# Attention in an encoder layer: probabilities turned in pairs of key blocks, four value products in a row, two banks for the summed output

## The reference

```python
def one(qblk):
    s = jnp.einsum('bqhd,bkhd->bhqk', qblk, k, preferred_element_type=jnp.float32) * scale
    p = jax.nn.softmax(s, axis=-1).astype(v.dtype)
    return jnp.einsum('bhqk,bkhd->bqhd', p, v)
...
a = _dense_attention_blocks(q, k, v)
mla_out = a.reshape(B, S, MLA_WIDTH) * jax.nn.silu(mg)
```

## Time and profile before

| | |
|---|---|
| median of 3 executions | 2474.99 us (2474.07 to 2484.44) |
| the profiled execution | 2480.64 us, of which 2478.5 us are its span |
| TensorE matmul, busy | 2292.8 us, 93% of the span |
| TensorE weight load | 1895.0 us, 76% |
| VectorE | 1399.8 us, 56% |
| ScalarE | 1137.2 us, 46% |
| GpSimd | 1020.0 us, 41% |
| DMA | mean 109 GB/s |
| TensorE's granted clock, mean | 0.975 of full speed |

### The profile page before, as it was taken

How to read it: one execution, slowest core, us unless ns; L and a number is a source line. 1 busy time by engine, 2 the same in 40 slices (tenths; PEclk the granted TensorE clock), 3 DMA queues, 4 the chain that set the end, 5 groups by cost and what they waited for, 6 DMA issues and landing times. The chain is left out here.

```text
span 2478.5 us, 34465 instructions
## 1 busy us (share of the span) xinstructions
PE 2292.8 (93%) x11362; PEld 1895.0 (76%) x11362; DVE 1399.8 (56%) x2120; ACT 1137.2 (46%) x2119; POOL 1020.0 (41%) x754
## 2 busy tenths in 40 slices
PE   1999999999996999999999889988999999996998
PEld 1888878898884787777778668877878888775786
DVE  8333335444345777776777631124888888764342
ACT  3544433222224555555555525553556555552332
POOL 5322222222223333232332212231888988873453
PEclk9999999999998999999999989999999999997999
DMA  7443324343435333333423223330111111124553
GB/s 283 146 151 127 127 84 159 122 144 128 148 118 142 97 109 97 102 97 95 111 84 94 94 99 118 127 110 19 43 52 60 60 58 49 56 111 127 168 149 115
DMA packets 195091, 271.19 MB, mean 109 GB/s; under 512 B 10404, under 2 KB 137764, under 8 KB 190374
## 3 DMA queue, kind: packets, MB, share of 16 engines
q1 hardware_dynamic: 190374, 261.49, 32.9%
q10 hardware_dynamic: 4608, 8.39, 0.9%
HBM read 183.33 MB, written 86.51 MB: 109 GB/s over the span
## 5 line engine op out<-in xcount | busy, mean ns | idle before, releaser
L2141 POOL TENSOR_TENSOR conv_g<-conv_g,product 128x1024 f32<-128x1024 f32 x160 | 380.3, 2413 | 44.8 <-ACT product L2180 44.8
L2270 DVE SCALAR_TENSOR_TENSOR ps_b<-u,cols,ps_b 128x1024 f32<-128x1024 f32 x304 | 364.7, 1281 | 0.0
L2330 PE MATMUL ps_a<-ho_hi,wp_lo 128*128 128x512 f32 x768 | 308.9, 402 | 21.6 <-DVE h_left L2289 6.4
L2332 PE MATMUL ps_a<-ho_hi,wp_hi 128*128 128x512 f32 x768 | 305.9, 398 | 0.0
L2331 PE MATMUL ps_a<-h_left,wp_hi 128*128 128x512 f32 x768 | 303.8, 396 | 0.0
L1424 ACT ACTIVATE pt_hi<-ps_pt 128x512 fp32r<-128x512 f32 x256 | 154.1, 603 | 220.3 <-PE ps_pt L1625 218.8
L1536 DVE TENSOR_TENSOR pt_lo<-ps_pt,pt_hi 128x512 fp32r<-128x512 f32 x256 | 175.6, 687 | 130.5 <-ACT pt_hi L1424 118.2
L2180 ACT ACTIVATE product<-u,cols 128x1024 f32<-128x1024 f32 x160 | 181.2, 1149 | 132.3 <-POOL conv_g L2141 126.5
L1526 DVE TENSOR_REDUCE mx<-ps_s 128x1 f32<-128x512 f32 x256 | 173.0, 685 | 38.1 <-PE ps_s L1617 36.9
L2330 PEld LDWEIGHTS ps_a<-ho_hi,wp_lo 128*128 128x128 f32 x768 | 146.1, 190 | 57.7 <-DVE h_left L2295 7.7
L1417 ACT ACTIVATE probs<-ps_s,bias 128x512 f32<-128x512 f32 x256 | 174.0, 698 | 30.1 <-DVE bias L1532 22.5
(11 more groups left out here) (389 smaller groups left out, 5602.0 us busy)
## 6 DMA issues: line engine op xcount, KB each, us to landing
scratch_ret_pack<-pack SPq DMA_DIRECT2D x14, 1280.0 KB, 5.5
pack<-scratch_ret_pack SPq DMA_DIRECT2D x14, 1280.0 KB, 6.5
k_st<-scratch_k_t SPq DMA_DIRECT2D x64, 256.0 KB, 3.5
v_st<-scratch_v SPq DMA_DIRECT2D x64, 256.0 KB, 3.8
ada<-in_ada_w_dram SPq DMA_DIRECT2D x16, 768.0 KB, 6.1
wp_raw<-in_od_w_in_dram SPq DMA_DIRECT2D x24, 512.0 KB, 3.9
xt<-in_x_dram SPq DMA_DIRECT2D x16, 512.0 KB, 5.9
ada<-in_ada_w_dram SPq DMA_DIRECT2D x8, 1024.0 KB, 7.0
```

Source lines behind the costliest of these rows:

```text
L2141: pool.tensor_tensor(half(conv_g, h), half(conv_g, h), product[h][:], ALU.add).then_inc(added, 1)
L2270: ins = dve.scalar_tensor_tensor(acc[h], units(c, k, h), w, acc[h], ALU.mult, ALU.add)
L2330: pe.matmul(dst, lo[:, k, :], h_hi[:, k, t], start=k == 0, stop=False)
L2332: mm = pe.matmul(dst, hi[:, k, :], h_hi[:, k, t], start=False, stop=k == KD - 1)
```

## The change

In a block TensorE had turned one key block after score set 0, one after set 1, and after sets 2 and 3 came two value products, a turn, a product, a turn, a product. Now the block is: score sets 0, 1, 2; two turns; score set 3; four value products; two turns. The products that use a block's last two turns run in the next block, as before. ScalarE and VectorE follow in their orders. The two banks `ps_ot` and `ps_turn` become two banks `ps_ot`, used by the groups in turn; a group's output is turned back into the bank it was summed in, and the first value product of a group waits until VectorE has read the bank's last contents (`out_ready`) instead of the copy (`o_out`).

```diff
--- before.py
+++ after.py
@@ -1254,8 +1254,7 @@
 
         ps_s = [bank(f"ps_s{i}") for i in range(4)]
         ps_pt = [bank(f"ps_pt{i}") for i in range(2)]
-        ps_o = bank("ps_ot")
-        ps_turn = bank("ps_turn")
+        ps_o = [bank(f"ps_ot{i}") for i in range(2)]
 
         v_in = [sem(f"v_in{i}") for i in range(QB)]
         qlo_first = sem("qlo_first")
@@ -1332,9 +1331,8 @@
         def left_over(n, b, values, write):
 
             if b < 2:
-                return (n - 2, NK - 5 + 4 * b) if write else None
-            return (n - 1, 4 * (b - 2) + 3) if values else None
-
+                return (n - 2, NK - 6 + 4 * b) if write else None
+            return (n - 1, 4 * (b - 2) + 2) if values else None
 
         QUARTERS = ((0, 1), (2,), (3,), ())
 
@@ -1431,8 +1429,15 @@
                             exps(n, s, b - 1, i)
                         if b == 0 and values:
                             exps(n - 1, 1 - s, 3, i)
-                        if i == 0 and left_over(n, b, values, write):
-                            turn_hi(*left_over(n, b, values, write))
+                    late = left_over(n, b, values, write)
+                    if late:
+                        turn_hi(late[0], late[1])
+                        turn_hi(late[0], late[1] + 1)
+                    if score and not last(n, 1):
+                        if values and b == 0:
+                            act.wait_ge(s_done, 16 * n)
+                        for q in QUARTERS[b]:
+                            split_k(n + 1, 1 - s, q)
                     if turned:
                         turn_hi(turned[0], turned[1])
                         turn_hi(turned[0], turned[1] + 1)
@@ -1440,14 +1445,7 @@
                         act.wait_ge(pv_done, 16 * (n - 1))
                         if not isinstance(n, int) or n > 2:
                             act.wait_ge(o_turned, n - 2)
-                        act.activation(o_t[:], ps_o[:], ACT.Copy).then_inc(o_out, 1)
-                    if score and not last(n, 1):
-                        if values and b == 0:
-                            act.wait_ge(s_done, 16 * n)
-                        for q in QUARTERS[b]:
-                            split_k(n + 1, 1 - s, q)
-                    if turned:
-                        turn_hi(turned[0], turned[1] + 2)
+                        act.activation(o_t[:], ps_o[s][:], ACT.Copy).then_inc(o_out, 1)
                     for k in w_steps(n, b):
                         act.wait_ge(wo_in[k], 16)
                         if k == 0:
@@ -1539,8 +1537,7 @@
             def group(n, s, score, values, write):
                 for b in range(QB):
                     turned = turned_in(n, b, values, write)
-                    if left_over(n, b, values, write):
-                        turn_lo(*left_over(n, b, values, write))
+                    late = left_over(n, b, values, write)
                     if b == 3 and score:
                         hold(dve, st, ada_in, 16 * (n + 1))
                         half = slice(s * 3 * D // 2, (s + 1) * 3 * D // 2)
@@ -1553,12 +1550,12 @@
                     for i in range(4):
                         if score:
                             block_max(n, b, i)
-                        if i < 2 and turned:
-                            turn_lo(turned[0], turned[1] + i)
+                        if i < 2 and late:
+                            turn_lo(late[0], late[1] + i)
                         if i == 3 and score:
                             block_bias(n, b)
-                        if i == 3 and turned:
-                            turn_lo(turned[0], turned[1] + 2)
+                        if i >= 2 and turned:
+                            turn_lo(turned[0], turned[1] + i - 2)
                         if b == 1 and i == 0 and values:
 
                             hold(dve, st, exp_done, 16 * n)
@@ -1579,7 +1576,7 @@
                         hold(dve, st, gate_in, 16 * (n - 1))
                         hold(dve, st, inv_done, n - 1)
                         for qb in range(QB):
-                            ins = dve.scalar_tensor_tensor(gate[:, qb, :], ps_turn[:, qb * P:(qb + 1) * P], inv[s][:, qb:qb + 1],
+                            ins = dve.scalar_tensor_tensor(gate[:, qb, :], ps_o[s][:, qb * P:(qb + 1) * P], inv[s][:, qb:qb + 1],
                                                            gate[:, qb, :], ALU.mult, ALU.mult)
                         ins.then_inc(out_ready, 1)
 
@@ -1625,15 +1622,15 @@
                     mm = pe.transpose(ps_pt[kt % 2][:, qb * P:(qb + 1) * P], probs[sl][qb][:, kt * P:(kt + 1) * P], ident)
                 mm.then_inc(pt_done, 1)
 
-            def values_of(m, kt):
+            def values_of(m, sl, kt):
                 pe.wait_ge(ptlo_done, 16 * m + kt + 1)
                 if kt % 4 == 0:
                     pe.wait_ge(vlo_done, 4 * m + kt // 4 + 1)
-                if kt == 0:
-                    pe.wait_ge(o_out, m)
-                pe.matmul(ps_o[:], v_lo[:, kt, :], pt_hi[kt % 4][:], start=kt == 0, stop=False)
-                pe.matmul(ps_o[:], v_hi[:, kt, :], pt_lo[kt % 4][:], start=False, stop=False)
-                pe.matmul(ps_o[:], v_hi[:, kt, :], pt_hi[kt % 4][:], start=False, stop=kt == NK - 1).then_inc(pv_done, 1)
+                if kt == 0 and not (isinstance(m, int) and m < 2):
+                    pe.wait_ge(out_ready, m - 1)
+                pe.matmul(ps_o[sl][:], v_lo[:, kt, :], pt_hi[kt % 4][:], start=kt == 0, stop=False)
+                pe.matmul(ps_o[sl][:], v_hi[:, kt, :], pt_lo[kt % 4][:], start=False, stop=False)
+                pe.matmul(ps_o[sl][:], v_hi[:, kt, :], pt_hi[kt % 4][:], start=False, stop=kt == NK - 1).then_inc(pv_done, 1)
 
             def group(n, s, score, values, write):
                 for b in range(QB):
@@ -1646,32 +1643,27 @@
                     def values_next(d):
 
                         if turned and turned[1] + d >= 0:
-                            values_of(turned[0], turned[1] + d)
+                            values_of(turned[0], s if b == 0 else 1 - s, turned[1] + d)
                         elif b == 1 and write and d < 0:
-                            values_of(n - 2, NK + d)
+                            values_of(n - 2, s, NK + d)
 
                     if score:
                         scores(n, s, b, 0)
+                        scores(n, s, b, 1)
+                        scores(n, s, b, 2)
                     turn_next(0)
-                    if score:
-                        scores(n, s, b, 1)
                     turn_next(1)
                     if score:
-                        scores(n, s, b, 2)
                         scores(n, s, b, 3)
 
-                    values_next(-2)
-                    values_next(-1)
+                    for d in range(-2, 2):
+                        values_next(d)
                     turn_next(2)
-                    values_next(0)
                     turn_next(3)
-                    values_next(1)
                     if b == 1 and write:
                         pe.wait_ge(o_out, n - 1)
-                        if not isinstance(n, int) or n > 2:
-                            pe.wait_ge(out_ready, n - 2)
                         for qb in range(QB):
-                            mm = pe.transpose(ps_turn[:, qb * P:(qb + 1) * P], o_t[:, qb * P:(qb + 1) * P], ident)
+                            mm = pe.transpose(ps_o[s][:, qb * P:(qb + 1) * P], o_t[:, qb * P:(qb + 1) * P], ident)
                         mm.then_inc(o_turned, 1)
 
             over_groups(pe, group)
```

## The result

The changed kernel takes **2509.56 us** (median of 4 runs, 2506.50 to 2510.53), the kernel before 2474.84 (4 runs of the same comparison, 2474.07 to 2484.44): a ratio of 1.0129, 95% interval 1.0103 to 1.0155. It is slower by 34.7 us. The forecast was 2496 in a range of 2470 to 2518.

A forecast was written before the change was run, and what follows sets the result against it. TensorE was taken to set attention's pace, with 1.43 us of waits a group. Loop groups +28.6, straight groups +2.6, group 1 +1.5, seams -7 and attention's end -5 gave +20.7: 2496 us on the median, range 2470 to 2518.

The forecast's parts named there:

- Two banks: A group's first value product, V(0), stops waiting for the output copy, part of 1.43 us of waits a group; price nothing.
- VectorE's rows and T1: A block's second turn waits for the previous block's last low part: 0.17 us in three blocks, 1.08 in block 1.
- VectorE's rows and V(1): The fourth value product waits for a low part now behind the bias: 0.4 us a block in the loop, ends 0 and 0.6.
- T3 behind V(1): The block's last turn, moved behind the fourth value product, delays the new group's exponentials in block 0: loss 1.18 us a group.
- A group in the loop: One group inside the loop with all its losses: 41.4 us, 2.86 above 38.55; ten groups +28.6 us.
- Group 1: It has no earlier products to put ahead of its fourth value product, which waits for the whole bias chain: +1.5 us.
- The loop's seam: VectorE's pause between loop passes costs TensorE 4.5 us instead of 11.6, as VectorE finishes its pass earlier: -7 us.
- The end of attention: In the blocks without scores, copies of the output weights come earlier: 1.7 us a block, -5 us, ends -9 and 0.
- Rival 1: The delay chains cost in the loop what they cost in straight code: 2474 us, no change; chance 0.13.
- Rival 2: VectorE's low parts reach the fourth value product and second turn in time everywhere: faster, 2453 us; chance 0.07.
- Rival 3: TensorE's clock falls after the new waits, 1.7 us a group in 14 groups: 2520 us; chance 0.08.
- Rival 4: The pause between loop passes moves along with VectorE's last row, so nothing is saved there: 2503 us; chance 0.10.

The follow-up runs named there:

- e1: Changed kernel with VectorE's low part of a block's second turn moved from behind the bias to ahead of the fourth maximum: 2491.71 us.
- e2: Changed kernel with both low parts of the previous block's last two turns moved ahead of the first maximum on VectorE: 2493.17 us.
- e3: Changed kernel with the fourth value product moved behind the block's last two turns on TensorE: 2486.70 us.
- e5: Changed kernel with the VectorE orders of e1 and e2 together, and the second pair of turns between the second and third value products: 2452.17 us.
- e4: Kernel before with the two output banks alone, turns and products in their old order: 2476.61 us, ratio 0.9991.
- e12: Kernel before with the ten groups of its loop written out straight: 2466.93 us, ratio 0.9955.
- e8: Changed kernel with the five passes of its loop written out straight: 2477.72 us, ratio 1.0001 to the kernel before.
- e10: e4 with ScalarE's copy of the output moved behind the third high part of block 1: 2471.78 us, ratio 0.9976 to the kernel before.
- e6: e5 with its second pair of turns split by a value product: 2456.21 us, ratio 0.9905 to the kernel before.

## Why the prediction was right

Slower was right, the mechanism too: the three delays that it named are there, and each went from its place when its cause was taken away (e1, e2, e3), T1's with a part of it back at V(1). The sum was +20.7 against 25.9 between the profiled executions. By its steps:

- **Turns in pairs**, 37.04 for a group without waits: e5 has 37.15. The base of the changed group is 41.82 less its losses, 37.19.
- **Two banks**, "price nothing": right for the change (e5). But the 1.43 was not to be had by the banks: e4 took V(0)'s wait away and won nothing.
- **VectorE's rows and T1**: 0.17 in three blocks was 0.28, 0.23 and 0.15, and 1.08 in block 1 was 1.08: 1.74 a group, forecast 1.59. e2 moved it.
- **VectorE's rows and V(1)**, the most uncertain price at 0.4 a block: 0.45, 0.44, 0.43, 0.37, in all 1.69 for 1.6. e1 took it away and won 1.69.
- **T3 behind V(1)**: 1.20, forecast 1.18. e3 took the wait back to 0.2.
- **A group in the loop** 41.82 for 41.4, ten times +3.27 for +2.86: 4 us, the largest miss of the sum. **Straight** 39.4 for 39.2: four times +0.92 for +0.65. The changed kernel has both, inside its loop and outside it.
- **Group 1**, +1.5: V(1) there waits 1.00 for the bias chain, as said. From the first score matmul to the first turned output are 89.07 (773.81 to 862.88) where they were 87.21 (775.37 to 862.58): +1.9, and +1.8 between e12 and e8.
- **The loop's seam**: 3.2 in one execution and 5.2 in another, forecast 4.5, before 11.6. The pause is still there: 3.0 to 4.3 us at the four seams, and 3.5 to 4.6 in the second execution, against 2.9 to 5.0 before. But 2.8 to 2.9 of it VectorE would wait for scores in any case, as it does at the same place in e8. The clock may have a part as well: before, behind waits of TensorE of 2.5 and 3.0 us, it was granted at 0.88 of full speed around the second seam (1076 to 1090) and at 0.91 around the third (1157 to 1175), with 1.00 around the other two, and with the change it is 1.00 around all four. How much of the saving this is, no run separates.

```profile
1174.64 0.39 PE L1614 MATMUL ps_s<-k_hi,q_hi 128*128 128x512 f32 x1
...
1177.97 0.65 PE L1622 MATMUL ps_pt<-const,probs 128*128 128x128 f32 x4 [0.62 <-DVE pt_lo L1534]
1179.17 0.66 PE L1622 MATMUL ps_pt<-const,probs 128*128 128x128 f32 x4 [0.54 <-DVE pt_lo L1534]
```

```profile
1171.89 0.42 DVE L1510 CAST v_hi<-v_st 128x512 fp32r<-128x512 f32 x1
1176.63 0.69 DVE L1524 TENSOR_REDUCE mx<-ps_s 128x1 f32<-128x512 f32 x1 [4.32 <-PE ps_s L1614]
```

TensorE, then VectorE, at the costliest of the seams (its group took 43.45). The maximum is put down to a wait for scores, but these were done at 1174.64 + 0.39 = 1175.03, and a maximum follows its scores by 0.15; it started 1.45 later than that. This is the seam, and behind it two turns wait 0.62 and 0.54 for the low parts. Neither e8 nor e12, without a loop, has such a group. The rule from the Trainium skill's page "Advanced Engine Details and Errata", section "Control Flow Timing" (51 ns for a branch, 108 ns for a compare-and-branch), would have given the seam next to no price; the runs disagree, with 3.2 to 11.6 us over the four seams, by where the pause falls.

- **The end of attention**: -5 was -3.1 (60.07 from the last turned output but two, before 63.21).
- **The sum**, read from row to row: attention starts 1.56 earlier than in the execution before, ahead of anything that the change touches (-1.56); then come +1.86 to the first turned output, +26.99 from there to the last but two, -3.14 to the last one, and +1.75 behind attention, where TensorE waits 3.32 for a load of `mix_e` instead of 1.68. That makes 25.90. The first and the last of these are in no term of the forecast, and they cancel by chance. The wait for `mix_e` is 1.2 to 3.4 in the other runs, 3.11 in e4 and 1.24 in e8, so it is not the pairs' doing. Attention alone costs 25.7 where the forecast had 20.7.

Of what was to show it, one sign failed: TensorE's listed waits on VectorE were to grow by 15 to 25 us and grew by 9.2 (22.1 + 9.0 against 18.7 + 3.2). The losses of T1 inside a joined record (1.31 above instead of 1.04) and the slow restarts are in no list of waits; the distances of the rows are what counts.

Rival 1 (straight-code prices) did not happen. e8 shows its prices in a kernel, with groups of 39.37 for its 39.2; that e8's 2477.72 is near the 2474 of rival 1 says less, because e8 has no seams and rival 1 kept 4.6 us of them. Rival 2 fell, because V(1) is 0.37 to 0.45 late in every block. Rival 3 fell, because the clock is 1.00 from 870 to 1400 us. Rival 4 fell with seams of 3.2 and 5.2 instead of 11.6.

## What to carry to other kernels

When an order is regrouped, write down for each engine which rows now stand behind a wait that they don't need; here two such places on VectorE (one ahead of the first maximum, one ahead of the fourth) and one on TensorE (T3) made 4.6 us a group, and moving those rows turned a loss of 1.3% into a gain of 1.1%. A wait of one engine is worth only what the next chain leaves: before taking one away, find what would be late without it (e4 won nothing, e10, with the row behind it moved too, 0.56 a group). And take durations of short dependent rows from inside the loop that is to run them.

## What the runs showed of the hardware

- The same rows on VectorE stand further apart inside this loop than in code written out: from maximum to low part 1.37 against 0.99 us. In the loop each wait also takes its value from the counter and has an increment of its own behind it, and no run tells these from the loop itself. With e8 this was worth 2.4 us a group, with e5 nothing, since its rows have slack.
- Between two passes of the loop VectorE starts nothing for 2.9 to 5.0 us in the kernel before (4.53 in the earlier trace rows, where the same place without a seam takes 0.12, 1118.84 to 1118.96); whether that costs anything is set by the work that TensorE still has.
- Eight transposes in a row take 1.03 us from the first one's start to the last one's end, 0.79 to the next matmul's start. Changing over between turns and products costs TensorE at most 0.01 us a time (e6, whose groups outside the loop are at most 0.03 longer for four changes more), although the record behind a turn is 0.48 long instead of 0.39.
